# Differential attention: the score maximum taken map by map at five of 32 steps, and a key tile moved ahead of the last map's transposes

## The reference

```python
    def one_block(args):
        qb, bi = args
        ...
        s = jnp.einsum('bhmqd,bhmkd->bhmqk', qb, kh) * scale
        s = jnp.where(allowed, s, -jnp.inf)
        p = jax.nn.softmax(s, axis=-1)
        a = p[:, :, 0] - lam * p[:, :, 1]
        return jnp.einsum('bhqk,bhke->bhqe', a, vh)
...
    kv = mem_n @ w_kv
    k = kv[..., :D_MODEL].reshape(B, M, CROSS_HEADS, CROSS_DH)
```

## Time and profile before

| | us |
|---|---|
| median of 3 runs (lowest, highest) | 832.19 (832.10, 832.24) |
| the profiled execution's own time | 832.24 |
| its span in the trace | 830.5 |
| PE busy | 814.6 |
| DVE busy | 587.0 |
| ACT busy | 437.8 |

### The profile page before, as it was taken

How to read it: one execution, slowest core, us unless ns; L and a number is a source line. 1 busy time by engine, 2 the same in 40 slices (tenths; PEclk the granted TensorE clock), 3 DMA queues, 4 the chain that set the end, 5 groups by cost and what they waited for, 6 DMA issues and landing times.

```text
span 830.5 us, 13216 instructions
## 1 busy us (share of the span) xinstructions
PE 814.6 (98%) x4586; PEld 683.7 (82%) x4586; DVE 587.0 (71%) x1360; ACT 437.8 (53%) x1057; POOL 83.6 (10%) x123
## 2 busy tenths in 40 slices
PE   7999999999999999999999999999999999999997
PEld 6887888888788888878888898888888888888885
DVE  6788668767578667767857877599845564367997
ACT  7865445445445445445545666543655464356543
POOL 3100122210000111111100000000010000001201
PEclk9999999999999999999999999999999999999999
DMA  9321359972144245655512168955331121206945
GB/s 295 107 82 39 108 169 190 183 135 73 33 134 112 77 80 98 124 96 121 109 61 83 59 192 244 280 156 141 126 103 60 56 64 39 90 13 134 215 96 202
DMA packets 70410, 99.21 MB, mean 119 GB/s; under 512 B 6597, under 2 KB 38473, under 8 KB 70345
## 3 DMA queue, kind: packets, MB, share of 16 engines
q1 hardware_dynamic: 52360, 64.29, 24.4%
q0 software_dynamic: 15392, 29.36, 19.6%
q10 hardware_dynamic: 2592, 4.72, 1.8%
HBM read 83.68 MB, written 31.46 MB: 139 GB/s over the span
## 4 chain that ended last, share of the span: by engine, by line
PE 92%; DVE 5%; ACT 1%; issue 1%; DMA 0%; POOL 0%; ACTq 0%; DVEq 0%
PE bank L1842 14%; PE bank L1844 14%; PE bank L1843 14%; PE banks2to L1842 10%; PE banks2to L1844 10%; PE banks2to L1843 10%; PE banks6to L1914 4%; PE banks2to L2101 3%; PE bank L2124 2%; DVE neg_max L1641 2%; PE banks2to L2037 1%; PE bank L2126 1%; PE banks6to L2061 1%; DVE w_lo L1380 1%; PE banks6to L1844 1%
## 5 line engine op out<-in xcount | busy, mean ns | idle before, releaser
L1844 PE MATMUL bank<-w_hi,actT_lo 128*128 128x512 f32 x412 | 161.3, 391 | 0.0
L1842 PE MATMUL bank<-w_hi,actT_hi 128*128 128x512 f32 x384 | 154.8, 403 | 0.3
L1843 PE MATMUL bank<-w_lo,actT_hi 128*128 128x512 f32 x384 | 149.6, 390 | 0.0
L1380 DVE SCALAR_TENSOR_TENSOR w_lo<-w_raw,vecs,w_hi 128x512 fp32r<-128x512 f32 x120 | 86.8, 750 | 43.3 <-ACT w_hi L1098 43.3
L1844 PEld LDWEIGHTS bank<-w_hi,actT_lo 128*128 128x128 f32 x412 | 77.3, 188 | 16.9
L1098 ACT ACTIVATE w_hi<-w_raw,vecs 128x512 fp32r<-128x512 f32 x120 | 82.5, 719 | 8.3 <-DMA w_raw<-in_w_ckv 4.2
L1842 PEld LDWEIGHTS bank<-w_hi,actT_hi 128*128 128x128 f32 x384 | 73.0, 190 | 15.1 <-DVE w_lo L1380 1.5
L1843 PEld LDWEIGHTS bank<-w_lo,actT_hi 128*128 128x128 f32 x384 | 72.3, 188 | 13.4
L984 POOL TENSOR_TENSOR rs_o<-var_o,neg_half 128x1 f32<-128x1 f32 (+1 forms) x48 | 28.9, 602 | 379.3 <-DVE var_o L1668 256.9
L1844 PE MATMUL banks2to<-w_hi,actT_lo 128*128 128x512 f32 x164 | 64.0, 390 | 0.0
L1263 ACT ACTIVATE prob<-banks2to,neg_maxs 128x128 f32<-128x128 f32 (+7 forms) x64 | 47.0, 741 | 15.2 <-DVE neg_maxs L1642 15.0
(11 more groups left out here) (368 smaller groups left out, 2045.1 us busy)
## 6 DMA issues: line engine op xcount, KB each, us to landing
w_raw<-in_w_in SPq DMA_DIRECT2D x56, 256.0 KB, 3.2
out_sums<-in_w_out POOLq DMA_DIRECT2D x11, 1024.0 KB, 9.7
late_sums<-in_w_co POOLq DMA_DIRECT2D x11, 1024.0 KB, 9.2
w_raw<-in_w_ckv SPq DMA_DIRECT2D x32, 256.0 KB, 3.5
w_raw<-in_w_cq SPq DMA_DIRECT2D x32, 256.0 KB, 2.8
stage_in<-in_x SPq DMA_DIRECT2D x8, 512.0 KB, 4.6
tile_a<-mixed ACTq DMA_DIRECT2D x16, 256.0 KB, 3.3
x_res<-in_x SPq DMA_DIRECT2D x8, 512.0 KB, 6.1
```

The costliest lines, as they stand in the source:

```text
L1380: return dve.scalar_tensor_tensor(dst, src, scale, hi.bitcast(F32), ALU.mult, ALU.subtract)
L1842: pe.matmul(dst, l_hi, r_hi, start=start, stop=False)
L1843: pe.matmul(dst, l_hi, r_lo, start=False, stop=False)
L1844: return pe.matmul(dst, l_lo, r_hi, start=False, stop=stop)
```

## The change

At steps 6, 14, 22, 30 and 31 (`MAX_SPLIT`) `max` reduces map 0 alone, and a new stage `max2` reduces map 1 behind the low parts of the previous step's transposes. `E` is cut into `E` (map 0) and `E2` (map 1), which for these steps waits for `max2`. `MT 0 0` goes from the middle of proj 41 to behind it. `K 2` goes ahead of `T 31`, and `comb 31` and `pvvar 30` behind `Ke 1` and `PV 30`.

```diff
--- before.py
+++ after.py
@@ -91,6 +91,7 @@
 SLOT, SLOT_BEFORE = weight_slots()
 
 PROJ_SPLIT = [GLA_STEPS + n for n in (1, 2, 3, 4, TT + 4, 2 * TT + 4, 3 * TT + 4)]
+MAX_SPLIT = [6, TT + 6, 2 * TT + 6, DIFF_STEPS - 2, DIFF_STEPS - 1]
 SIDE_BANK = [GLA_STEPS + n for n in (1, 3, TT + 4, 2 * TT + 4, 3 * TT + 4)]
 
 
@@ -156,37 +157,42 @@
 
     last = DIFF_STEPS - 1
     n_turned = 0
-    plan.extend([("S", 0), ("max", 0), ("E", 0), ("comb", 0)])
+    plan.extend([("S", 0), ("max", 0), ("E", 0), ("E2", 0), ("comb", 0)])
     plan.extend([("proja", GLA_STEPS + 2), ("TQK", 1), ("proj", GLA_STEPS + 2)])
     for i in range(last):
         plan.append(("S", i + 1))
         plan.append(("max", i + 1))
-        plan.extend([("pvvar", i - 1)] if i else [])
+        late = i + 1 in MAX_SPLIT
+        plan.extend([("pvvar", i - 1)] if i and not late else [])
         plan.extend(turned_maps(i))
         split = GLA_STEPS + i + 3 in PROJ_SPLIT
         if i + 2 < DIFF_STEPS and not split:
             plan.append(("TQK", i + 2))
+        plan.extend([("max2", i + 1), ("pvvar", i - 1)] if late else [])
         plan.extend([("pvfin", i - 1)] if i else [])
-        plan.extend([("E", i + 1), ("comb", i + 1)])
+        plan.append(("E", i + 1))
+        if i + 1 < last:
+            plan.extend([("E2", i + 1), ("comb", i + 1)])
         plan.extend([("loadm", 0, 0), ("loadm", 1, 0)] if i == DIFF_STEPS - TT - 4 else [])
         if split:
             plan.extend([("proja", GLA_STEPS + i + 3), ("TQK", i + 2)])
         if i + 3 < DIFF_STEPS:
-            if i + 3 > DIFF_STEPS - TT and not split:
+            first_tile = i + 3 == DIFF_STEPS - TT + 1
+            if i + 3 > DIFF_STEPS - TT + 1 and not split:
                 plan.append(("proja", GLA_STEPS + i + 3))
                 plan.extend(turned_tile(n_turned))
                 n_turned += 1
             plan.append(("proj", GLA_STEPS + i + 3))
-            if i + 3 > DIFF_STEPS - TT and split:
+            if first_tile or (i + 3 > DIFF_STEPS - TT and split):
                 plan.extend(turned_tile(n_turned))
                 n_turned += 1
         if i == last - 2:
             plan.extend([("Ka", 0), ("PV", i), ("K", 0), ("Ke", 0)])
         elif i == last - 1:
-            plan.extend([("K", 1), ("Ke", 1), ("PV", i)])
+            plan.extend([("K", 1), ("Ke", 1), ("E2", last), ("PV", i), ("K", 2), ("comb", last)])
         else:
             plan.append(("PV", i))
-    plan.extend([*turned_maps(last), ("pvvar", last - 1), ("K", 2), ("pvfin", last - 1), ("Ke", 2)])
+    plan.extend([("pvvar", last - 1), ("Ke", 2), *turned_maps(last), ("pvfin", last - 1)])
     plan.extend(turned_tile(n_turned))
     n_turned += 1
     plan.extend([("K", 3), ("Ke", 3), *turned_tile(n_turned), ("PV", last), ("pvvar", last), ("pvfin", last)])
@@ -321,7 +327,7 @@
 
         n = place[stage]
         if stage[0] == "proj" and stage[1] > GLA_STEPS:
-            while plan[n][0] != "E":
+            while plan[n][0] != "E2":
                 n += 1
         elif stage[0] == "proj" and stage[1] % TT < TT - 1:
             ends = ("o",)
@@ -369,7 +375,7 @@
             if where == ("proj", GLA_STEPS + DIFF_STEPS - 2):
                 where = before[-3]
             elif where == ("proj", GLA_STEPS + DIFF_STEPS - 1):
-                where = ("E", DIFF_STEPS - 3) if k == early else ("TQK", DIFF_STEPS - 1)
+                where = ("E2", DIFF_STEPS - 3) if k == early else ("TQK", DIFF_STEPS - 1)
             elif k >= early and where[0] == "proj" and GLA_STEPS < where[1] < GLA_STEPS + DIFF_STEPS - 1:
                 i = where[1] - GLA_STEPS - 3
                 where = ("PV", i) if k == early else ("T", i + 1, (i + 1) % TT // 4)
@@ -437,6 +443,7 @@
 SPLIT = rings({"Ke", "V", "Qe"})
 MIXED = rings({"O"})
 SPLIT_Y = rings({"ya"})
+MAXED = {stage: n + 1 for stage, n in rings({"max", "max2"}).items()}
 SUMMED_Y = {stage: n for n, stage in enumerate(
     stage for stage in PLAN if stage[0] == "ysum" and stage[1] in ("s3", "s2"))}
 
@@ -1251,20 +1258,19 @@
                         act.wait_ge(w_dve, X_W0 + 16)
                     hi, _, ps = ring_job(stage)
                     copy(hi, ps).then_inc(ring_act, 1)
-                elif kind == "E":
+                elif kind in ("E", "E2"):
                     i = w[0]
                     n = P * (i % TT + 1)
-                    act.wait_ge(s_max, i + 1)
-                    if i:
+                    m = int(kind == "E2")
+                    act.wait_ge(s_max, MAXED[("max2" if m and i in MAX_SPLIT else "max", i)])
+                    if i and m == 0:
                         act.wait_ge(ring_pe, TR[("T", i - 1, (i - 1) % TT // 4)] + 1)
-                    for m in range(2):
-                        if m and i == DIFF_STEPS - 1:
-                            act.wait_ge(s_max, i + 2)
-                        last = act.activation(
-                            prob[:, m, 0:n], wide[:, 2 * m:2 * m + 2, :].rearrange("p j c -> p (j c)")[:, 0:n],
-                            ACT.Exp, scale=DQK ** -0.5, bias=neg_maxs[:, i % 2, m:m + 1],
-                            accum_out=exp_sum[:, i % 2, m:m + 1])
-                    last.then_inc(s_act, 1)
+                    last = act.activation(
+                        prob[:, m, 0:n], wide[:, 2 * m:2 * m + 2, :].rearrange("p j c -> p (j c)")[:, 0:n],
+                        ACT.Exp, scale=DQK ** -0.5, bias=neg_maxs[:, i % 2, m:m + 1],
+                        accum_out=exp_sum[:, i % 2, m:m + 1])
+                    if m:
+                        last.then_inc(s_act, 1)
                 elif kind == "PV":
                     i = w[0]
                     act.wait_ge(pv_sum, i + 1)
@@ -1632,15 +1638,15 @@
                     hi, lo, ps = ring_job(stage)
                     dve.wait_ge(ring_act, TURN_ACT[stage] + 1)
                     lo_part(lo, ps, hi).then_inc(ring_dve, 1)
-                elif kind == "max":
+                elif kind in ("max", "max2"):
                     i = w[0]
                     n = P * (i % TT + 1)
                     dve.wait_ge(s_pe, i + 1)
                     both = wide[:, :, :].rearrange("p (m j) c -> p m (j c)", m=2)[:, :, 0:n]
-                    for m in [slice(0, 1), slice(1, 2)] if i == DIFF_STEPS - 1 else [slice(0, 2)]:
-                        then_wait(dve.tensor_reduce(neg_max[:, i % 2, m], both[:, m, :], AX.X, ALU.max, negate=True))
-                        dve.tensor_scalar(neg_maxs[:, i % 2, m], neg_max[:, i % 2, m], DQK ** -0.5, None,
-                                          ALU.mult).then_inc(s_max, 1)
+                    m = slice(1, 2) if kind == "max2" else slice(0, 1 if i in MAX_SPLIT else 2)
+                    then_wait(dve.tensor_reduce(neg_max[:, i % 2, m], both[:, m, :], AX.X, ALU.max, negate=True))
+                    dve.tensor_scalar(neg_maxs[:, i % 2, m], neg_max[:, i % 2, m], DQK ** -0.5, None,
+                                      ALU.mult).then_inc(s_max, 1)
                 elif kind == "comb":
                     i = w[0]
                     j = i % 2
```

## The result

| | before | after |
|---|---|---|
| median of 11 runs (lowest, highest), us | 832.07 (831.95, 833.23) | 834.18 (833.91, 834.55) |
| the profiled execution's own time | 832.24 | 834.18 |
| its span | 830.5 | 832.4 |
| PE busy | 814.6 | 815.5 |

The ratio is 1.0024, with a 95% interval of 1.0015 to 1.0033: the change is slower by 0.24%, just beyond the 0.2% that I took as the limit, and the interval has that limit inside it. 833.0 was forecast. The result is 1.2 above that, and 0.1 above the top of the range.

What follows compares the result with a forecast made beforehand. The prediction took PE, busy 814.6 of 830.5 us, to bound the kernel. Its terms -1.05 - 0.53 + 2.4 = +0.8 us on the profiled 832.24 gave a forecast of 833.0, range 830.9 to 834.1.

Steps and rivals of the forecast that it cites:

- The term of -1.05: Steps 6, 14 and 22: the split removes a projection stall of 0.35 at each, gaining 1.05 us.
- third rival: Head: late second exponential delays `qk_tok`, TQK 8, 16 and 24 wait, only 0.5 is gained: 834.1; chance 0.12.
- margin of 0.1: Step 6: `qk_tok` ends at 268.05, and TQK 8, which needs it, would start at 268.14, so it still fits.
- 0.3 of doubt: Uncertainty given to the head's gain, used with the tail's bounds for the likeliest case's spread.
- MT 0 0: Step 23: moved behind the whole projection, it finds `qkT_lo` done and gains 0.76 - 0.23 = 0.53 us.
- Steps 30 and 31: Tail: waits at S 31, K 1, K 2 and ahead of MT 7 0 make MT 7 0 start 2.4 us later.
- first rival: Step 30: S 31 is not held by the second exponential, MT 7 0 only +0.3, time 830.9; chance 0.13.
- second rival: Tail: evictions of T 31 are no wait, MT 7 0 comes 1.7 earlier, time 828.9; chance 0.08.
- Nothing waits behind MT 7 0: After MT 7 0: no PE wait depends on the change; weight tiles 65 to 68, their DMAs and K 4 shift with PE.
- The clock: Rival: PE's clock falls in the 1.8 wait before MT 7 0, K 3 takes 5.8, time 835.9; chance 0.02.
- the likeliest case: Whole kernel: the forecast of 833.0 itself, spread 832.0 to 834.2, chance 0.60.

Runs made afterwards that it cites:

- experiment 1: The changed kernel with the maximum of steps 6, 14 and 22 taken in one reduction again: 833.96 us, ratio 1.0020 to the kernel before.
- experiment 2: The kernel before, no split, with the two late `w` tiles of steps 6, 14 and 22 ahead of the transposes: 831.20 us, ratio 0.9988.
- experiment 5: The changed kernel, splits kept, with the two late weight tiles of steps 6, 14 and 22 ahead of the transposes: 834.27 us, ratio 1.0024.
- experiment 6: The changed kernel with steps 6, 14 and 22 unsplit and their two late weight tiles ahead of the transposes: 833.17 us, ratio 1.0010.
- experiment 3: The kernel before with MT 0 0 alone moved behind projection 41: 831.82 us, ratio 0.9995.
- experiment 7: The changed kernel with the maximum of step 30 taken in one reduction again: 833.12 us, ratio 1.0010 to the kernel before.
- experiment 4: The kernel before with the late weight tiles ahead of the transposes at steps 6, 14, 22 and MT 0 0 behind projection 41: 830.78 us, ratio 0.9983.
- experiment 8: The changed kernel with K 3 put between T 31 and MT 7 0: 837.14 us in 5 runs, ratio 1.0058 to the kernel before.
- experiment 9: As experiment 8, with weight tiles 69 to 71 behind the two mixed tiles' loads: 835.21 us, ratio 1.0040 to the kernel before.
- experiment 10: The changed kernel split only at step 31, with experiment 2's tile order, experiment 9's K 3 and tiles, and the tail reordered: 830.65 us, ratio 0.9980.
- experiment 11: As experiment 10, with PV 30's sum and square ahead of the late weight tiles: 831.14 us, ratio 0.9985 to the kernel before.
- experiment 12: As experiment 11, with step 30 split as well, its second reduction ahead of the two `w_lo`: 832.24 us, ratio 0.9999 to the kernel before.

## Why the prediction went wrong, point by point

**The head: wrong, and this is the step that failed.** I wrote that the late second exponential pushes `qk_tok` to 268.05, and that TQK 8, "which needs it", would start at 268.14: "it still fits, by 0.1". `qk_tok` did come as worked out: it ended at 267.63, which is 268.06 with the 0.43 of this profile added. But TQK 8 writes to bank 1, which PV 5, the last one ahead of it, has used, and so it waits for the sum of PV 5 as well, `pv_f`, the instruction that stands behind `qk_tok` on DVE. That ends at 267.97, 0.34 later; TQK 8 starts 0.14 behind it. The row of the kernel before was there to be read:

```profile
266.79 0.42 DVE L1662 TENSOR_REDUCE pv_f<-bank 128x128 f32<-128x256 f32 x1
```

It ends at 267.21. With the shift of 1.18 that I gave `qk_tok` this becomes 268.39, beyond the 268.14 at which TQK 8 was to start; measured are 267.97 + 0.43 = 268.40. The late second exponential isn't the only cause of the shift: it is over at 264.94, and `mix_out`, which waits 0.66 for POOL, at 264.88, just ahead of the combination at 264.97. The term of -1.05 measured +0.2. Experiments 1, 2, 5 and 6 show it from four sides: the splits alone lose 0.2 in the traces, the same stalls taken away without them gain 1.0, and with the tiles' better place the splits cost 1.1. This is my third rival ("the head gives nothing", 834.1, with a chance of 0.12), by its mechanism in all but the name of the instruction. The margin of 0.1 that I had computed should itself have made that chance larger, and the 0.3 of doubt that my bounds gave the head was a quarter of its error.

**MT 0 0: right.** Forecast 0.53, measured 0.60 in the trace, and 0.5 by the medians of experiment 3.

**Steps 30 and 31: right in mechanism and size.** The forecast was 20.2 from the maximum to MT 7 0, and 20.13 was measured, +2.35 for +2.4. Its steps hold one by one when the lead that PE really had, 0.84, is taken off the times that I gave on the scale of the kernel before:

| | forecast less 0.84 | measured |
|---|---|---|
| second maximum of step 30 scaled | 469.3 | 469.2 |
| S 31 | 470.5 | 470.50 |
| K 1 | 473.62 | 473.61 |
| PV 30 | 476.52 | 476.56 |
| K 2 | 478.78 | 478.73 |
| T 31 | 481.68 | 481.64 |
| MT 7 0 | 484.35 | 484.30 |

Experiment 7 splits the sum: 1.15 for the maximum of step 30, 1.2 for what the change does at step 31 (the places of K 2 and of the combination, which no run separates). The estimate for a reduction of 896, 1.09, was 1.08. The first and second rivals fell: S 31 was held, and the evictions of T 31 were a wait.

**Nothing waits behind MT 7 0: wrong, by 0.4 in the profiled execution.** I said that the weight tiles and their DMAs shift with PE. At the value tile's end they don't quite: 5.6 us went by from SP's issue to ACT's `w_hi`, and the same tile of the kernel before was issued at 511.49 and reached `w_hi` at 516.57, 5.1. Why the transfer took longer isn't settled. Experiments 1, 2 and 5 have the step too (0.7, 0.55 and 0.4), 3, 4, 6 and 7 don't. It doesn't follow from a late tail, for experiment 2 leaves the tail as it was and has PE 1.1 early there; its profiled execution is also the slowest of its 11 (831.71, median 831.20), so the step may come and go from execution to execution. No run was made to separate this, and the 0.4 isn't shown to be the change's.

**The clock: the rival fell for the changed kernel.** PE was busy for 0.38 us in the two ahead of MT 7 0, and the granted clock in that stretch is 1.00 (columns as in the earlier trace rows):

```profile
482.30:484.30 2.00, 0.38 (x5) 0.17 (x3) 1.77 (x4) 2.00 (x4) 0.00 (x0) 1.00 0.00 0
```

K 3's 24 matmuls behind it take 2.80 from first start to last, as K 2's 2.78 before the change. The fall that the Trainium skill ("TensorE: Matmul & The Clock Gate", section "What's actually happening") gives for an idle TensorE is not seen for a wait of this length. The page ties it to how long TensorE was idle, so my "by that rule this case would be real" took it too widely.

So the profiled execution is 1.1 above my sum: +1.25 at the head and +0.40 at the value tile, less 0.1 at MT 0 0 and in the tail together, and less the 0.43 that it was early at the start. That the 0.40 and the 0.43 cancel is luck, and so it is in part that the result lies within 0.1 of the 834.1 of my third rival, and just inside the 832.0 to 834.2 that I gave the likeliest case, although that case has the head wrong.

## What to carry to other kernels

Work out for a waiting instruction everything that it waits for, the bank's last reader too, and not only the operand in its name; here the second stood behind the first in one engine's queue and came 0.34 later. Splitting a reduction pays only where its second half and all that it pushes back have slack: here each of the splits at steps 6, 14, 22 and 30 gave back by a later hand-off at least what it had freed, and moving other work out of the way (the weight tiles) gained 1.0 us with no new instruction. The waits that were covered by moving work forward came back at the next resource (a weight's DMA, an issuing engine's queue): of experiments 8 to 12 none beat experiment 4, which leaves the tail alone, by more than 0.13.

## What the runs showed of the hardware

A maximum over PSUM costs DVE 1.08 us for 896 numbers, 1.22 for 1024, 2.02 for 1792 and 2.29 for 2048, in the traces of all fourteen kernels, wherever such a maximum occurs, to 0.015: about 1.04 ns a number and 0.15 for each instruction (an estimate from these four times). From the reduction's start to the next instruction behind the scaling it is 1.19 for one map of step 30 (467.95 to 469.14) and 2.14 for both at once (465.01 to 467.15), so a split itself costs DVE 0.24. A small step that goes from DVE to POOL and back (`var_o`, `rs_o`, `mix_out`) leaves DVE idle for 0.66 where it isn't covered, in the changed kernel as in experiment 12.
